# First products behind three norms taken from unnormalised activations, with the root and the shift applied to their outputs

## What the reference computes

```python
def rms_norm(x, g):
    y = x * lax.rsqrt(jnp.mean(x * x, axis=-1, keepdims=True) + NORM_EPS)
    return y * g

def modulate(x, g, shift, scale):
    return rms_norm(x, g) * (1 + scale) + shift

def swiglu(h, w1, w3, w2):
    return (silu(h @ w1) * (h @ w3)) @ w2

mod = silu(c) @ ada_w + ada_b              # 9 vectors of 1024
x = x + 0.5 * mod[0, 2] * swiglu(modulate(x, g[0], mod[0, 0], mod[0, 1]), ...)
x = x + mod[1, 2] * hybrid_mixer(modulate(x, g[1], mod[1, 0], mod[1, 1]), w_in, ...)
x = x + 0.5 * mod[2, 2] * swiglu(modulate(x, g[2], mod[2, 0], mod[2, 1]), ...)
```

## Time and profile before

| | |
|---|---|
| time, median of 3 runs (least to most) | 1995.74 us (1994.92 to 1996.67) |
| span of the profiled execution | 1992.7 us; its own time is not listed |
| instructions | 25487 |
| TensorE busy, weight loads busy | 98%, 78% |
| VectorE, ScalarE, GpSimd busy | 45%, 38%, 41% |
| mean data rate | 106 GB/s |

### The profile page before, as it was taken

How to read it: one execution, slowest core, us unless ns; L and a number is a source line. 1 busy time by engine, 2 the same in 40 slices (tenths; PEclk the granted TensorE clock), 3 DMA queues, 4 the chain that set the end, 5 groups by cost and what they waited for, 6 DMA issues and landing times.

```text
span 1992.7 us, 25487 instructions
## 1 busy us (share of the span) xinstructions
PE 1961.6 (98%) x9250; PEld 1552.8 (78%) x9250; DVE 901.8 (45%) x1457; ACT 747.8 (38%) x1241; POOL 825.9 (41%) x361
## 2 busy tenths in 40 slices
PE   7999999999999999999999999999999999999998
PEld 6877656688888888888888888776767878888887
DVE  6772565432632453457662204777872242101111
ACT  5343555432431232333313324436673243222321
POOL 4365321243554345435543443333444434443442
PEclk9999999999999999999999999999999999999999
DMA  6355111243656477548643343332123333333341
GB/s 180 88 142 134 32 44 43 55 102 102 169 155 192 122 186 201 138 118 212 172 105 95 84 116 71 78 75 53 33 54 76 94 75 94 101 100 95 86 115 53
DMA packets 154565, 211.14 MB, mean 106 GB/s; under 512 B 15432, under 2 KB 129640, under 8 KB 154344
## 3 DMA queue, kind: packets, MB, share of 16 engines
q1 hardware_dynamic: 140232, 167.34, 34.0%
q10 hardware_dynamic: 14240, 42.54, 7.1%
HBM read 206.69 MB, written 2.10 MB: 105 GB/s over the span
## 4 chain that ended last, share of the span: by engine, by line
PE 49%; issue 33%; POOL 14%; DVE 2%; DMA 1%; ACT 1%; POOLq 0%; ACTq 0%; SPq 0%; DVEq 0%
PE ps L670 15%; PE ps L672 15%; PE ps L671 15%; POOL wlo L620 13%; PE ps L1164 1%; PE ps L1188 1%; PE ps L769 1%; DMA xrow<-in_x 0%; DVE score L2384 0%; PE ps L787 0%; PE ps L1208 0%; DVE xT L2415 0%; PE ps L950 0%; PE ps L718 0%; DVE st L2006 0%
## 5 line engine op out<-in xcount | busy, mean ns | idle before, releaser
L620 POOL TENSOR_TENSOR wlo<-raw,whi 128x1024 fp32r<-128x1024 f32 (+1 forms) x317 | 779.8, 2475 | 1037.3 <-ACT whi L1458 1015.6
L670 PE MATMUL ps<-hhi,whi 128*128 128x512 f32 x1496 | 592.9, 396 | 7.6 <-POOL wlo L620 3.5
L672 PE MATMUL ps<-hhi,wlo 128*128 128x512 f32 x1496 | 584.2, 390 | 0.0
L671 PE MATMUL ps<-hlo,whi 128*128 128x512 f32 x1496 | 583.7, 390 | 0.0
L1458 ACT ACTIVATE whi<-raw 128x1024 fp32r<-128x1024 f32 x309 | 316.7, 1055 | 385.4 <-PE ps L672 359.6
L670 PEld LDWEIGHTS ps<-hhi,whi 128*128 128x128 f32 x1496 | 281.4, 188 | 75.5 <-issue 12.6
L672 PEld LDWEIGHTS ps<-hhi,wlo 128*128 128x128 f32 x1496 | 281.2, 188 | 59.5
L671 PEld LDWEIGHTS ps<-hlo,whi 128*128 128x128 f32 x1496 | 281.6, 188 | 56.7 <-issue 1.2
L670 PE MATMUL ps<-hidhi,whi 128*128 (+1 forms) x608 | 236.8, 390 | 0.0
L672 PE MATMUL ps<-hidhi,wlo 128*128 (+1 forms) x608 | 236.8, 389 | 0.0
L671 PE MATMUL ps<-hidlo,whi 128*128 (+1 forms) x608 | 236.8, 389 | 0.0
(11 more groups left out here) (401 smaller groups left out, 2353.5 us busy)
## 6 DMA issues: line engine op xcount, KB each, us to landing
raw<-in_ffn_w SPq DMA_DIRECT2D x264, 256.0 KB, 3.8
raw<-in_w_in SPq DMA_DIRECT2D x154, 256.0 KB, 4.0
trig<-in_ada_w ACTq DMA_DIRECT2D x72, 512.0 KB, 4.7
raw<-in_w_up SPq DMA_DIRECT2D x64, 256.0 KB, 4.0
raw<-in_w_down SPq DMA_DIRECT2D x64, 256.0 KB, 3.9
raw<-in_w_out SPq DMA_DIRECT2D x32, 256.0 KB, 3.7
xrow<-in_x ACTq DMA_DIRECT2D x4, 512.0 KB, 6.2
raw<-in_cmp_k_w SPq DMA_DIRECT2D x8, 256.0 KB, 3.7
```

The source lines that it names most:

```text
L620: last = pool.tensor_tensor(lo, src, hi.bitcast(F32), ALU.subtract)
L670: pe.matmul(out_, lhi, rhi, start=first, stop=False)
L671: pe.matmul(out_, lhi, rlo, start=False, stop=False)
L672: return pe.matmul(out_, llo, rhi, start=False, stop=last)
```

## The change

For norms 3, 4 and 5 TensorE does not wait for the normalised chunks. While the stage ahead ends, ScalarE also makes a high part of gain * x (`XHI`), VectorE its low part (`XLO`, `unscaled_low`); they lie in hidden buffers that are free then. The first unit of f1up0 and f2up0, and the first two blocks of fox, take these chunks, and the norm runs beside them. The root is copied to SBUF (`rstd`) by ScalarE, and the norm's 16 steps read it there. The outputs of the unnormalised products are multiplied with it by VectorE (`gates_scaled`, `first_chunks`, `first_queries`), and the shift enters as a bias: shift @ W for four output chunks, from an early copy of their weights (`early_w`, 2 MB for each norm in four DMAs on ScalarE's queue, `shift_weights`), 16 small steps of VectorE (`weight_shifts`), four products of one column (`shift_sums`) and copies (`biases`). These steps stand in the middle of the norm in the lists of VectorE and ScalarE, through hooks behind the chunks 1 and 3. GpSimd adds all squares (`squares`, seven adds in place of VectorE's), and one sum over channels replaces three. The products of `idle` are removed. In f1up0 `turn_modulation(4)` stands between the two halves of the shift's products. The core of the diff:

```diff
+        XHI = {3: chunks_at("xhi3", 8, 8), 4: chunks_at("xhi4a", 8, 2) + chunks_at("xhi4b", 20, 6), 5: chunks_at("xhi5", 16, 8)}
+        XLO = {3: chunks_at("xlo3", 40, 8), 4: chunks_at("xlo4a", 32, 2) + chunks_at("xlo4b", 52, 6),
+        wsum = t4("wsum", 0, 1)[:, 0, :]
+        WSUM = {3: wsum, 4: wsum, 5: Pb[:, 0, :]}
+        early_w = sb("early_w", [P, 4, SLAB], F32, HHI)
...
+            def squares(n):
+
+                e = STAT[n]
+                for m in range(1, KD):
+                    if m == KD - 1 and n == 3:
+                        low(AT[FIRST[n]] + 1)
+                    pool.wait_ge(n_sq, 8 * (e - 1) + m + 1)
+                    if m > 1:
+                        pool.wait_ge(n_add, 7 * (e - 1) + m - 1)
+                    pool.tensor_tensor(SQUARES[m], SQUARES[m - 1], SQUARES[m], ALU.add).then_inc(n_add, 1)
...
+            lows(AT["mixb1"] + SLOTS, AT["f1up0"] + 1)
+            squares(3)
+            lows(AT["f1up0"] + 2, AT["fox"] + 2)
+            squares(4)
+            lows(AT["fox"] + 2, AT["mixa2"] + SLOTS)
...
-                e = STAT[n]
-                if n:
-                    idle(n, 6 if n == 3 else 1)
-                    for x, m in enumerate((5, 6, 7)):
-                        if m == 5:
-                            pe.wait_ge(n_add, 5 * e)
-                        else:
-                            pe.wait_ge(n_sq, 8 * (e - 1) + m + 1)
-                        mm = token_sums(SQUARES[m], 0, x == 0, x == 2)
-                    mm.then_inc(n_sum, 1)
...
+            def square_sums(n):
+
+                pe.wait_ge(n_add, 7 * STAT[n])
+                token_sums(SQUARES[KD - 1], 6, True, True).then_inc(n_sum, 1)
+
+            def shift_sums(n, pair):
+
+                pe.wait_ge(ws_acc, 16 * (STAT[n] - 1) + 8 * pair + 8)
+                if pair:
+                    pe.wait_ge(bias_ready, 2 * (STAT[n] - 1) + 1)
+                for c in (2 * pair, 2 * pair + 1):
+                    mm = pe.matmul(ps[:, 6, 8 + c:9 + c], WSUM[n][:, P * c:P * c + P], ONES, start=True, stop=True)
+                mm.then_inc(ws_sum, 1)
...
+                                if unscaled and n == 1:
+                                    square_sums(4) if q == 0 else shift_sums(4, 0)
...
+                                    if unscaled and n == 1 and q == 0 and x == 4:
+                                        norm(4)
...
+                            if unscaled and n == 1:
+                                shift_sums(4, 1)
+                                pe.wait_ge(bias_ready, 2 * STAT[4])
...
+                                    elif isinstance(i, int) and i == 1:
+                                        pe.wait_ge(scaled, 4 * (STAT[nn] - 1) + 2 * w + c + 1)
...
+                                if unscaled and j == 2 and x == 4:
+                                    norm(nn)
+                                rhi, rlo = (XHI[nn][kk], XLO[nn][kk]) if unscaled else (hhi[:, kk, :], hlo[:, kk, :])
...
+                    blocks(0, True, {2: lambda: square_sums(nn), 3: lambda: shift_sums(nn, 0)})
+                    if f == 0:
+                        turn_modulation(4)
+                    shift_sums(nn, 1)
...
+                        if m == KD - 1 and len(late) == 3:
+                            high(late[0])
                         sc.wait_ge(x_ready, X_BEFORE_NORM[n] + m + 1)
+                        sc.activation(XHI[n][m], xT[:, m, :], ACT.Identity, scale=GAIN[n][:, m:m + 1]).then_inc(x_hi, 1)
                         sc.activation(SQUARES[m], xT[:, m, :], ACT.Square, scale=gtil[:, m:m + 1] if n == 3 else 1.0)\
...
+                    for s in late[-2:]:
+                        high(s)
                     sc.wait_ge(n_sum, e)
...
+                    if n != 4:
+                        sc.activation(early[:, n + 2:n + 3], col(C_EPS), ACT.Sigmoid)
+                    high(s0 + SLOTS)
+                    sc.wait_ge(n_all, e + 1)
+                    sc.activation(rstd[:, :], ps[:, 7, :], ACT.Copy).then_inc(rows_ready, 1)
...
+            def unscaled_query(v):
+
+                sc.wait_ge(scaled, 4 * (STAT[4] - 1) + v + 1)
+                sc.wait_ge(bias_ready, 2 * (STAT[4] - 1) + v // 2 + 1)
+                if v >= 2:
+                    sc.wait_ge(h_ready, 8 * H_NORM[4] + KD)
+                b = bias[:, v:v + 1]
+                sc.activation(SQ[v], tmp[:, v, :], ACT.Square, bias=b)
+                sc.activation(st[:, v, :], tmp[:, v, :], ACT.Identity, bias=b).then_inc(pj_ev, 1)
+
+            def first_queries():
+
+                unscaled_query(0)
+                unscaled_query(1)
+                high(AT["fox"] + SLOTS + 1)
...
+                    if name == "down1" and k == 1:
+                        shift_weights(3)
...
+                    s0 = AT[f"f{f + 1}up0"] + SLOTS
+                    high(s0 + 2)
+                    for c in range(2):
+                        sc.wait_ge(ff_m2, u0 + c + 1)
+                        sc.activation(hidhi[:, c, :], tmp[:, 2 + c, :], ACT.Copy).then_inc(ff_hi, 1)
+                    high(s0 + 3)
...
+            def first_gates(f):
+
+                e = STAT[(3, 5)[f]]
+                for c in range(2):
+                    sc.wait_ge(scaled, 4 * (e - 1) + c + 1)
+                    sc.wait_ge(bias_ready, 2 * (e - 1) + 1)
+                    sc.activation(tmp[:, c, :], st[:, c, :], ACT.Sigmoid, bias=bias[:, c:c + 1]).then_inc(ff_sig, 1)
+                high(AT[f"f{f + 1}up0"] + SLOTS + 1)
...
+                sc.wait_ge(w_used, AT[LAST_DOWN[n]])
+                for j in range(4):
+                    w, c = first[j // 2]
+                    src = w.rearrange("(k p) n -> p k n", p=P)[:, 4 * (j % 2):4 * (j % 2) + 4, c:c + 256]
+                    sc.dma_start(early_w[:, j, :].rearrange("p (k n) -> p k n", k=4), src).then_inc(ld_early, 16)
...
+            norm(3, [AT["down1"] + DOWN_K["down1"] - k + SLOTS for k in range(TAIL["down1"], 0, -1)], {1: lambda: first_gates(0)})
...
+            norm(4, [AT["f1down1"] + DOWN_K["f1down1"] - k + SLOTS for k in range(TAIL["f1down1"], 0, -1)], {3: first_queries})
...
+                    ve.wait_ge(rows_ready, STAT[n])
+                rows_of = ps[:, 7, :] if n == 0 else rstd[:, :]
...
+                                            in1=rows_of, op0=ALU.mult, op1=ALU.mult).then_inc(n_t, 1)
...
+                    if m in hooks:
+                        hooks[m]()
...
                 e = STAT[n]
+                ve.wait_ge(w_used, AT[LAST_DOWN[n]] + 1)
+                ve.wait_ge(ld_early, 64 * e)
+                for j in range(4):
+                    total = WSUM[n][:, 256 * (j // 2):256 * (j // 2) + 256]
+                        kk = 4 * (j % 2) + k
+                        w, c = early_w[:, j, 256 * k:256 * k + 256], SHIFT[n][:, kk:kk + 1]
+                        if kk == 0:
+                            ins = ve.tensor_scalar(total, w, c, None, ALU.mult)
+                        else:
+                            ve.wait_ge(ws_acc, 16 * (e - 1) + 4 * j + k)
+                            ins = ve.scalar_tensor_tensor(out=total, in0=w, scalar=c, in1=total, op0=ALU.mult, op1=ALU.add)
+                        ins.then_inc(ws_acc, 1)
...
+            def biases(n, pair):
+
+                x = 2 * (STAT[n] - 1) + pair + 1
+                ve.wait_ge(ws_sum, x)
+                ve.tensor_copy(bias[:, 2 * pair:2 * pair + 2], ps[:, 6, 8 + 2 * pair:10 + 2 * pair]).then_inc(bias_ready, 1)
+                ve.wait_ge(bias_ready, x)
+
+            def first_queries(pair):
+
+                for v in (2 * pair, 2 * pair + 1):
+                    g = G0["fox"] + v
+                    ve.wait_ge(*OUT_DONE[g])
+                    ve.tensor_tensor(tmp[:, v, :], ps[:, g % 4, :], rstd[:, :], ALU.mult).then_inc(scaled, 1)
+                biases(4, pair)
...
+            def gates_scaled(f):
+                    ve.tensor_tensor(st[:, c, :], ps[:, c, :], rstd[:, :], ALU.mult).then_inc(scaled, 1)
+                biases(n, 0)
...
+                for c in range(2):
+                    ve.scalar_tensor_tensor(out=tmp[:, c, :], in0=st[:, c, :], scalar=bias[:, c:c + 1], in1=tmp[:, c, :],
+                                            op0=ALU.add, op1=ALU.mult).then_inc(ff_m1, 1)
...
+            def first_chunks(f):
+                    ve.tensor_tensor(st[:, c, :], ps[:, 2 + c, :], rstd[:, :], ALU.mult).then_inc(scaled, 1)
+                biases((3, 5)[f], 1)
+                    ve.scalar_tensor_tensor(out=tmp[:, 2 + c, :], in0=st[:, c, :], scalar=bias[:, 2 + c:3 + c], in1=tmp[:, c, :],
+                                            op0=ALU.add, op1=ALU.mult).then_inc(ff_m2, 1)
+                    ve.tensor_tensor(hidlo[:, c, :], tmp[:, 2 + c, :], hidhi[:, c, :].bitcast(F32), ALU.subtract).then_inc(ff_ready, 1)
...
+            def unscaled_low(n, m):
+                ve.wait_ge(x_hi, 8 * (STAT[n] - 1) + m + 1)
+                ve.scalar_tensor_tensor(out=XLO[n][m], in0=xT[:, m, :], scalar=GAIN[n][:, m:m + 1],
```

(11 more changed lines are left out.)

168 lines of the change are left out of this document (107 added, 61 removed).

## The result

The changed kernel takes 2001.95 us in the median of five runs (2001.41 to 2006.80), the kernel before 1995.74. The ratio is 1.0037, with an interval from 1.0025 to 1.0049: slower, by some 0.4%. The profiled execution's span is 1999.9 us, 7.2 above the one of before.

A forecast was written before the change was run, and what follows sets the result against it. TensorE, busy for 98% of the span, was taken as the bound. -4.4 (f2up0) + (4.6 + 1.4) (fox) + (3.6 + 1.0) (f1up0) = +6.2 us on a span of 1992.7, about 2002 as a time; range 1993 to 2008.

The forecast's parts named there:

- f2up0 -4.4: Second feed-forward's first stage: a gain of 4.4 us, bounds 2.8 and 6.0, with only small waits.
- fox +6.0: Stage fox: a loss of 4.6 us from TensorE standing 10.6 us for the second bias pair, plus 1.4 for the clock.
- f1up0 +4.6: First feed-forward's first stage: a loss of 3.6 us, TensorE standing nearly 9 us, plus 1.0 for the clock.
- T: The moment at which the last product of the stage ahead of a norm has been issued on TensorE.
- second bias: In fox, the second bias pair's copy on VectorE, ready at T + 35.1; TensorE is there at T + 24.5.
- hidden low parts: In f1up0, VectorE's low parts behind the norm, gates and scalings: through at T + 40.5 with waits.
- The chain behind: In f1up0, late adds, modulation steps, sigmoid and slab 8: 20.8 us before the change, 2.2 less after it.
- three late adds: In f1up0, VectorE adds that a split stretched to 4.62 us before the change; they may take 2.1 after it.
- A: Rival: f1up0's adds and modulation steps miss GpSimd's splits, -0.6 us in sum, 1995.1; slab 8's split before T + 55.5; chance 0.22.
- B: Rival: collisions of VectorE and GpSimd cost nothing anywhere, -5.9 us in sum, about 1990; chance 0.08.
- C: Rival: nothing waits in any of the three stages, -17.8 us, 1978; chance 0.04.
- D: Rival: early weight copies starve slab or modulation loads in the down stages, 2 us a norm on top, 2008; chance 0.08.

The follow-up runs named there:

- experiment 9: Changed kernel with norm 3 as before, fox without the second-bias wait, ScalarE's order there changed, and the forget gate ahead of the last two reciprocals: 1985.68 us.
- experiment 2: Changed kernel without TensorE's explicit wait for the second bias pair at the end of fox's second block: 1996.79 us.
- Experiment 10: Changed kernel with modulation steps 48 to 51 and their four loads left out, so the result differs: 1991.62 us.
- experiment 7: Changed kernel with the high part of fox's sixth slab, and so its GpSimd split, moved from the middle of the norm to behind it: 2000.02 us.
- experiment 1: Changed kernel with norms 3 and 4 put back to the code before, the change kept at norm 5 alone: 1990.34 us.
- Experiment 3: Changed kernel with 44 products whose result nothing reads put ahead of fox's wait for the second bias pair: 2000.19 us.

## Why the prediction was right

**The time.** 2002 was forecast, 2001.95 measured; with runs from 2001.41 to 2006.80 so close a hit is luck. The three parts are close too: f2up0 -4.4 against -4.7, fox +6.0 against +5.7, f1up0 +4.6 against +4.4. The signs that were named came as well: the waits of 9.8 us in fox, ended by VectorE, and of 8.6 us ahead of f1up0's third unit, ended by a split, and the clock of 0.50 behind both. In f1up0 the sum hides errors that cancel.

**TensorE's own work.** The squares were summed at T + 10.9 in fox (1232.54), as forecast; VectorE began at 1237.92, T + 16.3, and TensorE was through with its two blocks at T + 24.6. Most of what the array was to save if nothing waits is what experiment 9 gets at its two norms: 4.7 of 5.4 (8.06 - 2.7) at norm 5, 4.5 of 5.6 (8.34 - 2.7) at norm 4, there with two changes of order.

**fox.** The second bias was forecast for T + 35.1 and came at 1256.0, T + 34.4; the wait was 9.8, not 10.6. The clock behind it cost 1.6 to 1.8, not 1.4. That this wait makes most of the stage's loss is shown by experiment 2 (4.4 of 5.7). The prediction put every later product behind this wait, as the code has it, and did not ask whether they need it. They don't: the line orders nothing new, and behind it stood two more waits that the prediction does not name (the seventh slab, the forget gate).

**f1up0.** The hidden low parts were forecast for T + 40.5 and ended at 880.51, T + 39.9. The second slab, forecast 1.4 late, cost a wait of 0.7. The chain behind took 18.1 us (to 898.64), forecast 18.6, but otherwise than forecast. The three late adds were to take 2.1 and took 3.55, so they gave 1.1 of the 2.7 that the chain is shorter than before's 20.8; 0.95 came from their start (0.16 us of waiting for ScalarE's squares in place of 1.11) and 0.6 from the steps with their loads. So the third unit was 2.5 later than before counted from T (58.1 against 55.5), where 3.6 was forecast.

The clock was mis-sized: 1.0 was charged, with the next unit's slack, and the fourth unit (924.95) came 26.3 behind the third, before 23.5 (917.88), which is 2.8; the half clock until about 904.6 accounts for it. The rest of the stage is 0.9 shorter; 0.6 of this is a wait that before had at 940.5. The fourth unit's first product after and before, and that wait:

```profile
924.95 0.48 PE L701 MATMUL ps<-hhi,whi 128*128 128x512 f32 x1
...
917.88 0.50 PE L670 MATMUL ps<-hhi,whi 128*128 128x512 f32 x1
...
940.51 0.50 PE L670 MATMUL ps<-hhi,whi 128*128 128x512 f32 x1 [0.57 <-POOL wlo L620]
```

The misses cancel: +2.5 + 2.8 - 0.9 = +4.4 against 3.6 + 1.0 = 4.6. The mechanism, a late chain that ends in a slab's split, is the one that was forecast; that the sizes add up so well is luck.

The prediction counted the chain as late adds, modulation steps, sigmoid and slab; that some of its steps wait for loads which ScalarE issues only when a slot comes free is in before's trace as well (3.14 us ahead of 885.61), and was not named. Experiment 10 shows that the wait hangs on these steps and loads.

**f2up0.** Only waits under 1 us, as forecast. TensorE came to the second unit at 1652.45, T + 24.5 as forecast, and took 22.96 us over it, where 32 triples at 0.68 take 21.76: 1.2 us of small waits, 1.6 forecast. The upper bound of 6.0 was for none.

**The rivals.** A falls by its own sign, a third unit before T + 55.5: it came at T + 58.1. B falls with the low part that took 2.32 us beside a split and 0.75 without, so collisions cost something; experiment 7 puts the price of that one at 1.6. C falls with both long waits. D falls with experiment 1, and because TensorE waits no longer than before in the down stages ahead of the three norms.

**Port and clock.** The Trainium skill (SBUF — State Buffer, Who interferes with whom) has a step of VectorE with two inputs in SBUF contend with a step of GpSimd that reads SBUF, and calls the port pair that they share an exclusive lock. The rows agree: a low part took 2.32 us beside a split and ended 0.5 behind it, 0.75 without (experiment 7). The Trainium skill (TensorE: Matmul & The Clock Gate, HAM oscillation) has a stand make the array begin again at half rate, and would keep it busy. Experiment 3 agrees: products without a use kept the granted clock at 1.00, and the mean-square products took 1.8 us less.

## What to carry to other kernels

A normalisation can be moved behind the products that need it, and here each of two norms gave 4.5 to 4.7 us for it (experiment 9); but the work that is put there has to fit, so look first for the chain that already keeps level with TensorE, as the modulation steps of f1up0 did, and leave that place as it was. When a wait is taken away, list what its stand had covered: in fox a slab and a forget gate came due in its place, and only with their order changed too did the stage gain. A wait put in for a buffer's reuse may be implied already by the semaphores that lead to the next writer.

## What the runs showed of the hardware that was not expected

Two stands of nearly the same length cost differently behind them. After 8.6 us in f1up0 the granted clock was 0.50 from 898.64 to about 904.6, 2.8 us lost; after 9.8 us in fox it was 0.50 from 1256.07 to about 1259.5, 1.6 to 1.8 lost by experiment 3, and after 7.2 us at the same place in experiment 7 one more (the mean-square products of the next pair come 15.4 us behind the wait's end, 14.4 in the changed kernel). The start of the program, where the two kernels do the same, shows such a difference as well: a stand of 3.14 us before, with 0.50 until about 20.7, and one of 3.38 in the changed kernel, with 0.50 until about 23.9. What decides that was not tried.

```profile
18.52 0.77 PE L701 MATMUL ps<-hhi,whi 128*128 128x512 f32 x1 [3.38 <-DVE hlo L2120]
```

The stretch up to norm 3 differs by 1.4 us between two programs that do the same there (838.81 in before's profile, 840.23 in experiment 1's), and does so from the start on: the first product behind the first norm comes at 17.8 in the one and at 19.2 in the other. The changed kernel is 0.7 later at this product (18.52 against 17.82) and then has the longer stretch of half clock. For differences of this size spans have to be compared stage by stage.
